# Weight spreading through a widened copy on GpSimd, turn-wise side slots, and reordered natural-layout stores in a hybrid decoder step

## The reference, cut to what matters

```python
o_c, p_c = _nsa_compressed(...)        # 32-token blocks, softmax over 32 columns
o_s = ... _sel_attend(...)             # selected blocks (for this prompt length: all causal keys)
o_w = _window_banded(...)              # last 512 keys
y_A = gate_c * o_c + gate_s * o_s + gate_w * o_w      # per token and head, then times silu(z_A)
```

## Time and profile before

| | |
|---|---|
| time of the kernel, median of 3 runs | 941.55 us (941.21 to 942.39) |
| the profiled execution's own time | 941.44 us |
| its span in the trace | 939.6 us |
| TensorE (PE) busy | 888.7 us, 95% |
| VectorE (DVE) busy | 614.8 us, 65% |
| ScalarE (ACT) busy | 363.5 us, 39% |
| GpSimd (POOL) busy | 105.1 us, 11% |
| pairs stage | about 437 us to 695 us of the span |

### The profile page before, as it was taken

The page is one execution under the profiler, slowest core; times in us unless marked ns, Lnnn a source line. Parts: engine busy times, 40 slices in busy tenths (PEclk is TensorE's granted clock), DMA queues, the critical chain, the costliest instruction groups (busy, mean ns, idle before and its releaser), DMA issues.

```text
span 939.6 us, 15993 instructions
## 1 busy us (share of the span) xinstructions
PE 888.7 (95%) x6261; PEld 566.2 (60%) x6261; DVE 614.8 (65%) x1145; ACT 363.5 (39%) x786; POOL 105.1 (11%) x105
## 2 busy tenths in 40 slices
PE   6999999999999999998888989898999999999997
PEld 4656665666666666666666767576665666544443
DVE  4588889999788897997476685857644444322221
ACT  4211262110112201136677667765755656410111
POOL 0012110000010111101000322023132230000000
PEclk9999999999999999999999999999999999999999
DMA  8434642422134356523810000000029988432211
GB/s 306 162 135 163 217 157 57 60 59 72 45 113 173 132 170 220 187 83 90 320 68 1 3 1 2 1 2 1 2 76 395 358 315 329 177 117 89 78 52 50
DMA packets 32111, 118.34 MB, mean 126 GB/s; under 512 B 3434, under 2 KB 11772, under 8 KB 22972
## 3 DMA queue, kind: packets, MB, share of 16 engines
q0 software_dynamic: 9360, 68.16, 20.0%
q1 hardware_dynamic: 19053, 43.39, 13.1%
q10 hardware_dynamic: 3623, 5.76, 3.0%
HBM read 108.33 MB, written 13.29 MB: 129 GB/s over the span
## 4 chain that ended last, share of the span: by engine, by line
PE 73%; DVE 13%; DVEq 4%; issue 3%; ACT 2%; DMA 2%; SPq 2%; ACTq 0%
PE PS L834 27%; PE PS L2093 12%; PE PS L1624 5%; PE PS L1634 4%; PE PS L1654 4%; PE PS L810 3%; PE PS L1923 3%; PE PS L1944 3%; DVE main L607 2%; PE PS L1955 2%; PE PS L1978 2%; PE PS L1607 2%; DVE main L1472 2%; DVE main L604 1%; DMA main<-in_cmp_v_dram,row 1%
## 5 line engine op out<-in xcount | busy, mean ns | idle before, releaser
L834 PE MATMUL PS<-main 128*128 128x352 f32 (+1 forms) x1056 | 327.8, 469 | 0.0
L834 PEld LDWEIGHTS PS<-main 128*128 128x128 f32 x1056 | 200.3, 190 | 119.5 <-issue 1.3
L2093 PE MATMUL PS<-main 128*128 128x512 f32 x256 | 112.3, 593 | 0.1
L1430 ACT ACTIVATE main<-PS,main 128x512 f32<-128x512 f32 (+2 forms) x136 | 84.4, 628 | 67.6 <-DVE main L1459 42.2
L435 ACT ACTIVATE main<-PS 128x384 f32<-128x384 f32 x24 | 11.8, 490 | 205.4 <-PE PS L834 199.2
L1634 PE MATMUL PS<-cst,main 128*128 128x128 f32 x528 | 72.7, 281 | 18.9 <-ACT main L1428 8.9
L645 DVE SCALAR_TENSOR_TENSOR main<-main,par 128x1022 f32<-128x1022 f32 (+16 forms) x66 | 83.8, 1270 | 5.3 <-issue 0.4
L604 DVE TENSOR_TENSOR main<-main 128x1024 f32<-128x1024 f32 x64 | 75.4, 1220 | 9.6 <-DMA main<-in_cmp_k_dram,row 4.3
L2093 PEld LDWEIGHTS PS<-main 128*128 128x128 f32 x256 | 47.6, 190 | 56.4 <-issue 56.4
L607 DVE TENSOR_TENSOR main<-main 128x1024 f32<-128x1024 f32 (+2 forms) x96 | 75.0, 781 | 7.2
L1634 PEld LDWEIGHTS PS<-cst,main 128*128 128x128 f32 x528 | 56.8, 141 | 37.1 <-ACT main L1430 17.2
(11 more groups left out here) (324 smaller groups left out, 1047.8 us busy)
## 6 DMA issues: line engine op xcount, KB each, us to landing
main<-in_w_tiles_dram SPq DMA_DIRECT2D x24, 512.0 KB, 3.6
out_dram<-main SPq DMA_DIRECT2D x18, 256.0 KB, 2.1
main<-in_x_prompt_dram SPq DMA_DIRECT2D x8, 512.0 KB, 8.4
main<-in_w_out_dram SPq DMA_DIRECT2D x4, 1024.0 KB, 5.9
main<-in_x_prompt_dram SPq DMA_DIRECT2D x16, 256.0 KB, 3.0
out_dram<-main SPq DMA_DIRECT2D x4, 512.0 KB
diag<-in_win_k_dram SPq DMA_DIRECT2D x8, 256.0 KB, 8.3
diag<-in_win_v_dram SPq DMA_DIRECT2D x8, 256.0 KB, 7.3
```

Of the source, the lines that this page charges most:

```text
L834: last = pe.matmul(bank(3 * s + j)[:, 0:w], ring[:, s, k * P:(k + 1) * P], xT[:, k, t0:t0 + w], start=(k == 0), stop=(k == KD - 1))
L1430: last = act.activation(prob[:, k % 2, g, h * nk_ * P:(h + 1) * nk_ * P], score_set(k, g)[:, h * nk_ * P:(h + 1) * nk_ * P], ACT.Exp, scal ...
L2093: last = pe.matmul(out_bank(m, h), proj[:, MIX[k], n * P:(n + 1) * P], wo[:, k, h * 512:(h + 1) * 512], start=(x == 0), stop=(x == KD - 1))
```

## The change

1. A weight side is done in two steps. GpSimd copies the 8 weight columns 64 wide into a new SBUF buffer `wide` (128 x 512; `pool_wide`), and TensorE transposes `wide` with 4 transposes of 128 x 128. TensorE's wait for `w_ready` becomes one for `w_wide`. There is one such buffer; GpSimd fills it for weight side n+1 once TensorE has finished weight side n, and ahead of its addition for side n; after a tile's last side it does the addition and the gate first.
2. Weight sides get places of their own, behind the transposes (`turn`) of the first and of the second step in iteration b. The cmp sides stay behind the values' products. Some sides move to another iteration by it: batches 10, 11, 12, 14, 15, 16, 25, 27, 28, 31 and 35 hold two weight sides, 24 and 26 one; cmp sides stand in 10, 12, 13, 16, 24, 27, 30 and 34.
3. VectorE's loop in iteration b is now: part_out and cmp sides, both weight sides, row sums, weights, then both peaks of batch b+1, then gaps.
4. The natural stores go in three groups of four with a semaphore each (the old slots 3 and 4, then 5 and 2, then 0 and 1). part_out waits for the first group ahead of part 0 and for the second ahead of part 2; GpSimd waits for the second and third ahead of its first widening.

```diff
+        wide = carve(X0 + 2 * 9 * P + 4096, 512)
...
+        nat_out = [sem(f"nat_out{b}") for b in range(3)]
...
+            whole(3, 4, nat_out[0])
+            whole(4, 6, nat_out[0])
+            local(5, 10, nat_out[1])
+            whole(2, 2, nat_out[1])
+            whole(0, 8, nat_out[2])
+            local(1, 12, nat_out[2])
...
-        SLOTS = [(b, j) for b in range(1, len(BATCH) + 1) for j in range(len(BATCH[b - 1]))
-                 if not any(PART_OF[k] in SECOND for k in BATCH[b - 1])]
+        BY_VALUES = [(b, 0, j) for b in range(1, len(BATCH) + 1) for j in range(len(BATCH[b - 1]))
+                     if not any(PART_OF[k] in SECOND for k in BATCH[b - 1])]
         TAIL = len(BATCH) + 1
-        SLOTS += [(TAIL, j) for j in range(2 * R)]
-        SIDE, at_slot = [], 0
+        BY_VALUES += [(TAIL, 1, j) for j in range(2 * R)]
+        BY_TURN = [(b, 1, j) for b in range(1, len(BATCH) + 1) for j in range(len(batch(b)) or 2)] + [(TAIL, 1, j) for j in range(2 * R)]
+        SIDE, at_place = [], (0, 0, 0)
...
+                places = BY_VALUES if c is None else BY_TURN
+                at_place = next(x for x in places if x > at_place and x[0] >= done_batch(i) + (c is not None))
+                SIDE.append((at_place, i, "cmp" if c is None else "weight", c))
...
-                if n == 0:
-                    dve.wait_ge(SEM["nat_out"], 16 * N_NAT)
+                if n in (0, 2):
+                    dve.wait_ge(nat_out[n // 2], 64)
...
+            for b in range(TAIL):
+                for j, k in enumerate(batch(b - 1)):
+                    if k == PARTS[PART_OF[k]][3]:
+                        part_out(PART_OF[k])
+                        dve.drain()
+                    for m, item in enumerate(SIDE):
+                        if item[0] == (b, 0, j):
+                            dve_side(dve, m)
                 for m, item in enumerate(SIDE):
-                    if item[0][0] == b == TAIL:
-                        side(m)
+                    if item[0][0:2] == (b, 1):
+                        dve_side(dve, m)
                 for k in batch(b):
                     if k in SUMMED:
                         row_sums(k)
                 for i in ORDER:
                     if done_batch(i) == b:
                         weights(i)
-                for k in batch(b + 1)[:1]:
+                for k in batch(b + 1):
                     peak(k)
+                for i in ORDER:
+                    if i >= 4 and done_batch(i) - 1 == b:
+                        dve.drain()
+                        gaps(i)
+
+        WEIGHTS = [m for m, x in enumerate(SIDE) if x[2] == "weight"]
+
+        def pool_wide(pool, n):
+            m = WEIGHTS[n]
+            at_, i, kind, c = SIDE[m]
+            pool.wait_ge(SEM["w_ready"], ORDER.index(i) + 1)
+            if n == 0:
+                for stored in nat_out[1:]:
+                    pool.wait_ge(stored, 64)
+            else:
+                pool.wait_ge(SEM["side_ps"], WEIGHTS[n - 1] + 1)
+            one = weights_of(i)[:, c * 8:c * 8 + 8].rearrange("p (u o) -> p u o", o=1).to_broadcast([P, 8, HD])
+            pool.tensor_copy(wide.rearrange("p (u d) -> p u d", d=HD), one).then_inc(SEM["w_wide"], 1)
...
+            pool_wide(pool, 0)
+            for n, m in enumerate(WEIGHTS):
+                at_, i, kind, c = SIDE[m]
+                if m != LAST_SIDE[i]:
+                    pool_wide(pool, n + 1)
+                pool.wait_ge(SEM["side_sb"], m + 1)
...
+                pool.tensor_tensor(mixed(i), mixed(i), raw(i, c), ALU.add).then_inc(SEM["mixing"], 1)
+                if m == LAST_SIDE[i]:
...
+                    if n + 1 < len(WEIGHTS):
+                        pool_wide(pool, n + 1)
...
-                pe.wait_ge(SEM["w_ready"], ORDER.index(i) + 1)
+                pe.wait_ge(SEM["w_wide"], sum(x[2] == "weight" for x in SIDE[:m + 1]))
                 for r in range(R):
-                    for g in range(G):
-                        u = c * 8 + 2 * r + g
-                        last = pe.matmul(bank(7)[g * HD:(g + 1) * HD, r * P:(r + 1) * P], weights_of(i)[:, u:u + 1].to_broadcast([P, HD]), ident, start=True, stop=True)
+                    last = pe.transpose(bank(7)[:, r * P:(r + 1) * P], wide[:, r * P:(r + 1) * P], ident)
...
-                for k in batch(b):
-                    turn(k)
+                for j in range(2):
+                    for k in batch(b)[j:j + 1]:
+                        turn(k)
+                    for m, item in enumerate(SIDE):
+                        if item[0] == (b, 1, j) and b < TAIL:
+                            pe_side(pe, m)
```

More of the change, by code:

```diff
@@ L1444, in act_pairs, with dve_side @@
                     evac(k)
+        def dve_side(dve, m):
+            at_, i, kind, c = SIDE[m]
+            dve.wait_ge(SEM["side_ps"], m + 1)
+            if kind == "cmp":
+                if before(i) > 0:
+                    dve.wait_ge(SEM["oz"], before(i))
+                dve.tensor_copy(mixed(i), bank(7)).then_inc(SEM["side_sb"], 1)
+            else:
+                o = raw(i, c)
+                dve.tensor_tensor(o, o, bank(7), ALU.mult).then_inc(SEM["side_sb"], 1)
         def dve_pairs(dve):
@@ L1528, in weights @@
                 last.then_inc(SEM["w_ready"], 1)
-            def side(m):
-                at_, i, kind, c = SIDE[m]
-                dve.wait_ge(SEM["side_ps"], m + 1)
-                if kind == "cmp":
-                    if before(i) > 0:
-                        dve.wait_ge(SEM["oz"], before(i))
-                    dve.tensor_copy(mixed(i), bank(7)).then_inc(SEM["side_sb"], 1)
-                else:
-                    o = raw(i, c)
-                    dve.tensor_tensor(o, o, bank(7), ALU.mult).then_inc(SEM["side_sb"], 1)
             dve.wait_ge(strip_in, 16)
@@ L1545, in dve_pairs @@
             dve_prompt_turn(dve)
-            for b in range(TAIL + 1):
-                for j in range(2):
-                    if j < len(batch(b - 1)):
-                        k = batch(b - 1)[j]
-                        if k == PARTS[PART_OF[k]][3]:
-                            part_out(PART_OF[k])
-                            dve.drain()
-                        for m, item in enumerate(SIDE):
-                            if item[0] == (b, j):
-                                side(m)
-                    if j == 0:
-                        for k in batch(b)[1:] if b > 0 else []:
-                            peak(k)
-                        for i in ORDER:
-                            if i >= 4 and done_batch(i) == b:
-                                dve.drain()
-                                gaps(i)
+            for b in range(TAIL):
[6 more added lines that the diff above has]
+                            dve_side(dve, m)
                 for m, item in enumerate(SIDE):
-                    if item[0][0] == b == TAIL:
-                        side(m)
+                    if item[0][0:2] == (b, 1):
+                        dve_side(dve, m)
                 for k in batch(b):
@@ L1594, in pe_side @@
                 pe.wait_ge(SEM["side_sb"], m)
-            behind = [n for n in SECOND if B_OF[PARTS[n][2]] + 1 < at_[0]]
+            behind = [n for n in SECOND if B_OF[PARTS[n][2]] + 1 < at_[0] + at_[1]]
             if behind:
@@ L1748, in pool_decode @@
             pool.wait_ge(SEM["oz"], NT)
-            pool.wait_ge(SEM["nat_out"], 16 * N_NAT)
+            for stored in nat_out:
+                pool.wait_ge(stored, 64)
             for rnd in range(4):
@@ L1889, in gate @@
                 last.then_inc(SEM["dpair"], 1)
+            rest = list(TAIL_SIDES)
             dve.memset(sd[:, NEW + DS:NEW_W], 0.0)
@@ L1908, in dve_decode @@
                         gate(p - 1)
+                    if rnd == 0 and rest:
+                        dve_side(dve, rest.pop(0))
                     if r < 4:
@@ L2171, in _ @@
             sp.wait_ge(so_out, 16 * N_SO)
-            sp.wait_ge(SEM["nat_out"], 16 * N_NAT)
+            for stored in nat_out:
+                sp.wait_ge(stored, 64)
         @block.gpsimd
```

42 lines of the change are left out of this document (16 added, 26 removed).

## The result

| | before | after |
|---|---|---|
| median of the runs | 941.97 us (4 runs, 941.21 to 944.20) | 926.13 us (4 runs, 925.69 to 926.64) |
| ratio after / before, 95% interval | | 0.9828 (0.9810 to 0.9847) |
| profiled execution: time, span | 941.44, 939.6 us | 925.71, 923.7 us |
| PE busy | 888.7 us | 878.1 us |
| first scores of the stage to last scores | 682.09 - 436.62 = 245.5 us | 665.19 - 436.08 = 229.1 us |

The change makes the kernel 1.7% faster. The forecast was 926 us.

A forecast was written before the change was run, and what follows sets the result against it. PE was taken to bound the pairs stage, busy 219.9 of 244 us. From 941.4 us, stretch terms of -17.0 and +1.8 for GpSimd's copy gave 926.2, taken as 926; range 920 to 933.

The forecast's parts named there:

- iteration 3, stores: Pairs stage, iteration 3: the first part_out no longer waits for all twelve stores to land; -4.8 us.
- 7 and 22: Pairs stage, iterations 7 and 22: a part_out no longer stands between the two peaks; -1.4 us together.
- 11 to 13: Pairs stage, iterations 11 to 13: 22.8 us before, 20.9 with four cheaper weight sides and two cmp sides; -1.9 us.
- 24 to 26: Pairs stage, iterations 24 to 26: 1.9 us less PE work, and a 1.25 us wait goes; -3.1 us.
- 28 to 30: Pairs stage, iterations 28 to 30: a side with its wait (0.98 us) leaves the place between the peaks; -2.4 us.
- exposure of GpSimd's copy: Batches 10, 11, 12, 16, 25, 31: PE waits 0.3 us each for the one wide buffer's second copy; +1.8 us.
- A weight side: PE in the pairs stage: four transposes replace sixteen instructions, 0.48 instead of 0.95 us; 11.3 us over 24 sides where PE bounds.
- Order of the peaks: VectorE in the pairs stage: adjacent peaks shorten iterations they pace, by a side (0.69 and 0.29 us) or part_out (0.69).
- The new wait in 27: Iteration 27: PE's weight side waits for VectorE's cmp copy behind both peaks, 10.1 instead of 8.3 us; +1.8 us.
- that rival: Transposes lower TensorE's clock in the 14 iterations with weight sides, 2.3 us more in each; 958 us, chance 0.04.
- Everything after the stage keeps its length: Decode stage and everything later is chained on PE, so the pairs stage's gain is carried to the end; 0 us change.
- a sign of being wrong: Listed under what would show the forecast wrong: a decode stage that does not keep its length; no size given.

The follow-up runs named there:

- the second buffer: The changed kernel with cmp sides written earlier and two wide buffers used in turn for GpSimd's copies; 929.88 us, ratio 0.9836 to the kernel before.
- the last run above: The changed kernel with PE doing the first cmp side's products five times over, same result, so more PE instructions; 933.14 us, one run.

## Why the prediction was right, point by point

The total was right; the periods show which terms were.

| term | forecast | profile of after |
|---|---|---|
| iteration 3, stores | -4.8 | -4.83, but +1.3 in 0 and 1 |
| 7 and 22 | -1.4 | -1.9 |
| 10 | 0 | -0.15 |
| 11 to 13 | -1.9 | -1.7 |
| 14, 15 | -1.7 | -1.7 |
| 16, 17 | -2.1 | -2.1 |
| 24 to 26 | -3.1 | -3.4 |
| 27 | +1.8 | +1.3 (in later profiles up to +2.4) |
| 28 to 30 | -2.4 | -2.5 |
| 31 | -1.1 | -1.0 |
| 34, 35 | -0.3 | -0.6 |
| exposure of GpSimd's copy | +1.8 | in the rows above, some 0.4 |
| decode stage and output projection | 0 | +1.6 |

The others (8, 9, 23 and the stage's start) make -0.4.

- **Stores.** The mechanism was right, the size holds for the profile of before only. The wait ends when the stores land (460.35 to 463.44 us in four profiles), so it is worth what PE's arrival leaves of it. The runs give 2.5 us (stores alone) and 1.5 to 2.6 us (put back into the changed kernel), known to some 2 to 3 us, and the profiles 3.5 in the mean. In the profile of after this appears as the +1.3 us in iterations 0 and 1.
- **A weight side** was forecast at 0.48 us by counting transposes. The transposes take 0.43, and iteration 11 pays 0.55 a side with the stop ahead of the second one. The half price was right, but it holds only behind the turns; counting instructions missed the 0.15 us at each change of kind.
- **GpSimd's copy** was taken at 0.9 us, between bounds of 0.66 and 1.27; it takes 0.61, below both. With 0.35 us for the signals the forecast's own sum gives 0.61 + 0.35 - 0.95 = 0.01 us of waiting per pair; with the 0.86 us that the half turn between two sides takes it gives 0.10, and the second buffer shows 0.08. The Trainium skill (GPSIMD Engine Reference, Performance versus the Vector engine) gives 769 ns for 512 elements in a tight loop; the 611 ns measured for this copy is less.
- **Order of the peaks.** Iterations 11 to 17 and 24 to 31 came out to 0.3 us a row, but for 27 (0.5 us). The run with the peaks alone shows what the forecast did not say: this part is worth nothing by itself (1.0009), and the transposes by themselves only 3.2 us. Stores alone 2.5, transposes alone 3.2 and peaks alone -0.9 make 4.8 us, all together 16: some two thirds come from parts that need each other. Everything but the transposes gives 3.8 (0.996), of which the stores are 2.5. The new places have no run of their own.
- **The new wait in 27** came as forecast, with its cause: PE waits 1.29 us for the cmp side's copy behind both peaks. That the weights' operation takes 1.20 us beside GpSimd, here again at 618.92, is part of it.
- **The clock** did not fall: 1.00 in the stretches full of weight sides. The 2.3 us an iteration of that rival, and with it its 958 us, had no row behind it. The Trainium skill (TensorE: Matmul & The Clock Gate, Part 4, PE-mode transpose) says that the full clock does not engage for transposes; the trace disagrees.
- **"Everything after the stage keeps its length"** was wrong by 1.6 us in the profile of after; the prediction itself had named this as a sign of being wrong. The wait in the output projection, 1.5 us, is nearly all of it. By the packets' times (the last run above) it comes with the change: PE's code is shorter, and the border between two pieces of it fell on the third product. The forecast had no term for this. From the last scores to the last fold of the output projection the kernel before took 244.2 us and the changed one 245.2, 246.6 and 248.2 in its three profiles, and the experiments 244.7 to 248.9. The rest of this spread stands at the first exponentials of the decode stage, for which PE waits up to 2.7 us in profiles of either kind; what is late there was not settled.

That the medians agree to 0.1 us (926.13 for 926) is in part luck. In the profile of after the stage's other iterations gained 3.3 us more than forecast, 1.4 of it because the copy cost so little; against this stand 1.3 us less from the stores, counted with the slower start, and 1.6 us lost behind the stage.

## What to carry to other kernels

Write small PE jobs in the form of the block beside which they stand: the same four transposes cost 0.55 us among transposes and 0.70 among matmuls, and eight matmuls cost 0.95 among their like and 1.10 among transposes. A cheaper instruction, a new place and a new order in the queue of the engine behind it have to be tried together: the instruction alone was worth a fifth of the whole here, the order alone nothing, and everything without the instruction a quarter. A wait for something that the waiting engine doesn't set in motion (a store's landing) is worth its length less what the work ahead of it would lose anyway, and one profile doesn't show that; compare the absolute end in several. A change in the number of instructions can move a wait for code to a place far behind the change; look at the instruction queue's packets before a wait without a releaser.

## What the hardware showed that was not expected

- A change between a block of 64-wide matmuls and one of 128-wide transposes costs PE 0.15 us: 16 matmul instructions between transposes take 1.02 instead of 0.87 us, four transposes between matmuls 0.59 instead of 0.43. Some 0.1 of it shows in the block ahead of the change (the half block of values 1.02 instead of 0.92, 520.74 to 521.76 against 517.73 to 518.65 before). Whether the width of the weights or the operation counts, the runs don't separate.
- GpSimd copies 128 x 512 float32 from a broadcast column in 0.61 us, half of the 1.27 us of its addition of two operands and less than its memset's rate of 0.29 us for 224 columns.
- The same program starts the stage with a granted clock of 0.84 and 0.93 in one execution and 1.00 in another, behind the same 2.52 us of idle time; this moves iterations 0 and 1 by 1.2 us.
- PE goes on 1.23 to 1.38 us behind the end of a 16 KB packet of the queue that the profile calls "instruction", in nine profiles of nine with the same number of PE instructions, and stands still for up to 2.4 us there. All DMA together moves 348 GB/s meanwhile (790 to 792.2 us of after).
